# Two orders around the split of an input tile: the first three output tiles behind a norm, and the residual add of the norm behind a product

## The reference, cut to what matters

```python
h = rms_norm(x, mix_norm);  z = h @ w_in                      # product "z"
x = x + concat(o_gla, o_swa) @ w_out
h2 = rms_norm(x, ffn_norm); u = causal_dwconv(h2 @ w_up)      # product "upA"
...
u = rms_norm_2(h, mix_pre_g) @ w_pw1 + b_pw1                  # "pw1"
u = silu(layer_norm(conv(u))) @ w_pw2 + b_pw2                 # "pw2"
h = h + rms_norm_2(m, mix_post_g[layer])                      # post_norm
f = square(relu(rms_norm_2(h, ffn_pre_g[layer]) @ w_ff1)) @ w_ff2   # "ff1a0", "ff1a1"
h = h + rms_norm_2(f, ffn_post_g[layer])                      # post_norm
c_kv = rms_norm_2(rms_norm_2(h, kv_in_g) @ w_dkv, kv_norm_g)  # "dkv"
m = attention(...) @ w_o                                      # "wo"
```

## Time and profile before

| what | value |
|---|---|
| median of 3 runs | 1921.63 us (1921.1 to 1922.07) |
| span of the profiled execution | 1917.8 us |
| PE busy | 1813.4 us, 95% |
| PEld busy | 1462.6 us, 76% |
| DVE busy | 992.4 us, 52% |
| ACT busy | 628.4 us, 33% |
| POOL busy | 257.3 us, 13% |
| mean granted TensorE clock | 0.961 |

### The profile page before, as it was taken

One profiled execution on the slowest core, in us unless ns is written; L12 is line 12 of the kernel. 1 busy time (PEld: TensorE's weight loads), 2 busy tenths in 40 slices (PEclk: granted clock), 3 DMA queues, 4 the chain that ended last, 5 costly groups with the idle time before them and its releaser, 6 DMA issues.

```text
span 1917.8 us, 21982 instructions
## 1 busy us (share of the span) xinstructions
PE 1813.4 (95%) x8052; PEld 1462.6 (76%) x8052; DVE 992.4 (52%) x1290; ACT 628.4 (33%) x923; POOL 257.3 (13%) x216
## 2 busy tenths in 40 slices
PE   6999999999999999978999999988998999999996
PEld 5777978878888787857888788867666878878885
DVE  4575246663664399946542343365644374324433
ACT  4334134432343333434321222243323243112220
POOL 2100011110111122313210011120000131001111
PEclk9998799999999999968999999999889999999998
DMA  4212023332232222302332222312200213222221
GB/s 176 78 55 67 1 88 107 98 120 89 87 98 94 72 92 84 110 22 78 99 99 92 94 89 97 99 44 88 88 0 1 77 57 108 99 90 96 92 84 44
DMA packets 43841, 156.01 MB, mean 81 GB/s; under 512 B 4864, under 2 KB 4992, under 8 KB 43776
## 3 DMA queue, kind: packets, MB, share of 16 engines
q1 hardware_dynamic: 43632, 154.19, 24.5%
q10 hardware_dynamic: 144, 0.92, 0.1%
HBM read 153.00 MB, written 2.10 MB: 81 GB/s over the span
## 4 chain that ended last, share of the span: by engine, by line
PE 74%; DVE 16%; ACT 5%; issue 4%; POOL 0%; ACTq 0%; DVEq 0%; DMA 0%; POOLq 0%; SPq 0%
PE bank L991 22%; PE bank L992 21%; PE bank L993 21%; DVE cv L1832 4%; DVE w_lo L1527 3%; DVE a_lo L1545 1%; PE bank L1475 1%; ACT w_hi L600 1%; ACT w_hi L590 1%; DVE h L1901 1%; DVE m L1894 1%; DVE tmp L1758 1%; PE bank L1059 1%; PE bank L1143 1%; PE bank L1478 1%
## 5 line engine op out<-in xcount | busy, mean ns | idle before, releaser
L991 PE MATMUL bank<-a_hi,w_hi 128*128 128x512 f32 x1252 | 503.3, 402 | 49.9 <-DVE w_lo L1527 19.7
L1527 DVE TENSOR_TENSOR w_lo<-w_raw,w_hi 128x1024 fp32r<-128x1024 f32 x283 | 367.6, 1300 | 317.8 <-ACT w_hi L590 192.7
L992 PE MATMUL bank<-a_lo,w_hi 128*128 128x512 f32 x1252 | 498.7, 398 | 0.0
L993 PE MATMUL bank<-a_hi,w_lo 128*128 128x512 f32 x1252 | 496.5, 397 | 0.0
L991 PEld LDWEIGHTS bank<-a_hi,w_hi 128*128 128x128 f32 x1252 | 239.5, 191 | 116.6 <-issue 20.4
L993 PEld LDWEIGHTS bank<-a_hi,w_lo 128*128 128x128 f32 x1252 | 239.7, 191 | 52.7
L992 PEld LDWEIGHTS bank<-a_lo,w_hi 128*128 128x128 f32 x1252 | 240.0, 192 | 50.9 <-issue 0.5
L991 PE MATMUL bank<-g_hi,w_hi 128*128 128x512 f32 x688 | 269.6, 392 | 4.7 <-DVE tmp L1924 3.3
L993 PE MATMUL bank<-g_hi,w_lo 128*128 128x512 f32 x688 | 269.9, 392 | 0.0
L992 PE MATMUL bank<-g_lo,w_hi 128*128 128x512 f32 x688 | 269.1, 391 | 0.0
L590 ACT ACTIVATE w_hi<-w_raw 128x1024 fp32r<-128x1024 f32 x167 | 173.7, 1049 | 161.4 <-PE bank L993 161.3
(11 more groups left out here) (272 smaller groups left out, 1900.8 us busy)
## 6 DMA issues: line engine op xcount, KB each, us to landing
w_raw<-in_stream SPq DMA_DIRECT2D x283, 512.0 KB, 3.4
h<-in_xT SPq DMA_DIRECT2D x8, 256.0 KB, 7.0
out<-h SPq DMA_DIRECT2D x8, 256.0 KB, 2.0
cst_b<-in_consts SPq DMA_DIRECT2D x1, 896.0 KB, 9.5
cst_b<-in_consts ACTq DMA_DIRECT2D x1, 896.0 KB, 4.5
cols<-in_vectors SPq DMA_DIRECT2D x1, 289.0 KB, 2.8
cst<-in_consts SPq DMA_DIRECT2D x1, 257.0 KB, 8.4
w_al<-in_w_alpha SPq DMA_DIRECT2D x1, 128.0 KB, 10.0
```

Source lines behind the costliest of these rows:

```text
L991: pe.matmul(out, w0, x0, start=start, stop=False, skip_group_check=loose)
L992: pe.matmul(out, w0, x1, start=False, stop=False, skip_group_check=loose)
L993: return pe.matmul(out, w1, x0, start=False, stop=stop, skip_group_check=loose)
L1527: dve.tensor_tensor(w_lo[slot][:, :], w_raw[slot][:, :], f(w_hi[slot][:, :]), ALU.subtract)\
```

## The change

Two orders are changed, no arithmetic instruction is added or removed.

In `three_tiles` PE waits for the high part of tile k, issues the two products with it (w_hi x x_hi, w_lo x x_hi) for all three output tiles, then waits for the low part, and issues the three products with it (w_hi x x_lo). The last matmul of each output tile is now one of these three, and `stat` comes behind the first of them.

In `post_norm`, at the places that feed an operand, the low part of tile k - 1 is made between the scaling of tile k and the residual add of tile k. The add still waits for the scaling.

```diff
                 for k in range(8):
-                    k_ready(split, k)
+                    pe.wait_ge(xhi_ready, SPLIT0[split] + k + 1)
+                    x0, x1 = x_tile(hi, lo, k)
                     for j in range(3):
                         if k == 0:
                             unit_ready(n0 + j)
                             bank_free(name, j)
                         slot = (n0 + j) % RING
-                        last = three(bank[j][:, :], T(w_hi[slot], k, P), T(w_lo[slot], k, P), *x_tile(hi, lo, k),
-                                     k == 0, k == 7)
+                        pe.matmul(bank[j][:, :], T(w_hi[slot], k, P), x0, start=(k == 0), stop=False)
+                        pe.matmul(bank[j][:, :], T(w_lo[slot], k, P), x0, start=False, stop=False)
+                    k_ready(split, k)
+                    for j in range(3):
+                        slot = (n0 + j) % RING
+                        last = pe.matmul(bank[j][:, :], T(w_hi[slot], k, P), x1, start=False, stop=(k == 7))
                         if k == 7:
                             last.then_inc(unit_used, 1)
...
-                    link(scale)
+                    if split and k:
+                        scale.then_inc(v_chain, 1)
+                        links[0] += 1
+                        x_lo(SPLIT0[split] + k - 1, a_lo, a_hi, k - 1, T(h, k - 1), col(next_gain, ng0 + k - 1))
+                        dve.wait_ge(v_chain, links[0])
+                    else:
+                        link(scale)
                     dve.tensor_tensor(T(h, k), T(h, k), T(m, k), ALU.add)\
                         .then_inc(h_ready if split else out_ready, 1)
-                    if split and k:
-                        x_lo(SPLIT0[split] + k - 1, a_lo, a_hi, k - 1, T(h, k - 1), col(next_gain, ng0 + k - 1))
```

## The result

| | before | after |
|---|---|---|
| median of 21 runs each | 1921.33 us (1912.55 to 1928.84) | 1930.81 us (1922.58 to 1939.09) |
| ratio | | 1.0061, 95% interval 1.0044 to 1.0077 |
| span of the first profile | 1917.8 us | 1921.1 us |
| spans of two further profiles (e7, e16; e8, e15) | 1919.7, 1922.6 us | 1928.2, 1924.0 us |

The change makes the kernel slower. By the ratio it is 0.61%, that is 11.7 us (8.5 to 14.8); the two medians lie 9.5 us apart, the two means 9.9. The forecast was 5.8 us: the sign is right, the size is some half of what came, and 1930.81 lies 0.8 us outside the range. The first profile shows only 3.3 us of it; with a mean clock (the granted TensorE clock as a share of full speed, over the span) of 0.964 it was one of the quickest executions of the new kernel.

A forecast was written before the change was run, and what follows sets the result against it. PE's queue and its standstills bound the kernel; +0.72 us at PE's places and +5.03 at the three norms made +5.8, so 1921.6 us became 1927.4. The range for 8 in 10 was 1918.5 to 1930 us.

The forecast's parts named there:

- who gets the port: At the three norms, POOL's sum asks 0.11 us before the residual add and goes first; the add waits 1.04 us.
- somewhat after its shown start: POOL's request for the port may come later than shown; if by over 0.11 us, the add wins.
- the first rival: At the norms the add gets the port first, tiles in pairs of 5.51 us: 1919.5 us in all; chance 0.28.
- z: Product "z": spread 0.91 us later, two matmuls left in k = 0 for 0.46 us: +1.37 us.
- pw2: Product "pw2": six matmuls run in PE's gap before the low part of tile 0: -1.37 us.
- pw1: Product "pw1": two matmuls left over after the third bank, plus the bare spread: +0.59 us.
- the change at PE, place by place: Prices three_tiles' new order at eight calls, without the norms' DVE chain: +0.72 us with the bare spread at "upA".
- upA: Product "upA": 0.13 us behind the stat is bare; the operand order does nothing else there.
- the three norms: "ff1a0" and "ff1a1" +1.72 us each, "dkv" +1.59, from tiles every 3.19 us and bare spreads: +5.03 us.
- what a sum of POOL costs an add: At the norms, a POOL sum falling wholly before a two-input DVE operation costs DVE 1.04 us.
- a rival of 0.07: The clock falls in the norms' new gaps, 2 to 4 us more each, near 1935 us; chance 0.07.

The follow-up runs named there:

- e7: The kernel before, unchanged, run once more for a second profile: 1921.50 us.
- e16: The kernel before, unchanged, run once more for a further profile: 1924.36 us.
- e8: The changed kernel, unaltered, run once more for a second profile: 1929.99 us.
- e15: The changed kernel, unaltered, run once more for a further profile: 1925.85 us.
- e3: Changed kernel with POOL's sums at the three norms cut to 8 of 512 columns: 1920.48 us, ratio 1.0014.
- e4: Kernel before with POOL's sums at the three norms cut to 8 of 512 columns: 1917.19 us, ratio 0.9992.
- e5: Changed kernel with a one-column memset ahead of each POOL sum at the three norms: 1935.94 us, ratio 1.0078.
- e14: Changed kernel with four one-column memsets ahead of each POOL sum at the norms, 128 columns allotted for them: 1921.46 us, ratio 1.0012.
- e1: Kernel before with the new order in three_tiles alone, post_norm as before: 1922.10 us, ratio 1.0020.
- e6: Kernel before with three_tiles' new order, except k = 0 of "z" and "pw1" and k = 7 before a stat: 1919.30 us, ratio 0.9998.
- e2: Kernel before with the new order in post_norm alone, three_tiles as before: 1931.34 us, ratio 1.0081.
- e13: Changed kernel with 72 unused SBUF columns (288 bytes a partition) allotted, no instruction added: 1954.71 us, ratio 1.0181.
- e12: Changed kernel with four one-column memsets ahead of each POOL sum at the norms, 72 columns allotted for them: 1945.08 us, ratio 1.0124.

## Why the prediction was right in sign and half in size

**Right: who gets the port.** The forecast rested on POOL's sum being shown 0.11 us ahead of the add. It is 0.10 to 0.11, the sum goes first in every tile, adds are 3.25 us apart (3.19 forecast) and PE waits for the high part from the fifth tile on (third or fourth forecast). Counted from the first add of the norm, PE's first matmul comes 1.3 us earlier (1.3 forecast) and the stat 2.8 us later (2.5). e3 against e4 gives the port 7.5 of the 9.2 us. That POOL asks "somewhat after its shown start", which made the rival 0.28, is bounded by e5 and e14: it wins at 0.06 us ahead and loses at 0.00 and at 0.03 behind. So the choice between the forecast and the first rival hung on 0.05 to 0.1 us. The Trainium skill, "SBUF — State Buffer", section "SBUF: two separate sides", has the first starter hold the shared port pair for the whole instruction; these runs agree, with 1.10 us added to an add of 0.69.

**Right: "z" and "pw2".** The spread of "z" waits 1.33 us for the reciprocal (0.40 before; 1.5 forecast). PE's timeline of the changed kernel:

```profile
40.06 1.16 PE L1059 MATMUL bank<-cst,r_tok 128*128 128x128 f32 x8 [1.33 <-DVE r_tok L1557]
```

At "pw2" six matmuls at half clock stand before a gap of 1.53 us in place of the 6.05; the stage is 2.98 us shorter, 1.5 without the change in half-clock time, 1.37 forecast. Of "pw1" (0.59 forecast, 1.31 measured) nothing can be said: 1.71 of it is the column of the half-clock time.

```profile
836.17 0.79 PE L1074 MATMUL bank<-a_hi,w_hi 128*128 128x512 f32 x1 [1.59 <-ACT a_hi L866]
...
840.63 1.65 PE L1079 MATMUL bank<-a_lo,w_hi 128*128 128x512 f32 x3 [1.53 <-DVE a_lo L1548]
```

**Failed: the list of places.** The step "*the change at PE, place by place*" took eight calls, and said of "upA" that 0.13 us is bare and "the operand order does nothing else". The ninth call, "wout", isn't behind a norm and has no stat, but its output feeds a chain of DVE's that is the bound up to "upA": four matmuls later for its first tile are 0.92 us more of waiting for PE, and the stage is 2.6 us longer with the half clock that followed (0.13 forecast). This is the one place that was left out altogether.

**Too small: the three norms.** 5.03 us were forecast, 6.54 stand in the three stages. The term that fell short is what a sum of POOL costs an add: 1.04 us in the forecast, from a low part of the old order, 1.10 measured. 0.06 us too little for each of six tiles (3.25, not 3.19) makes 0.36 a norm, 1.1 of the 1.5 in all. Behind "dkv" stand 1.05 more, as the next product starts with 3.41 us at half clock in all three profiles of the changed kernel and in one of before. It does so in e1 and e6 too and not in e2, so it isn't `post_norm`'s.

**Failed: the clock and the matmuls' distance were taken as fixed.** The prediction carried the clock as a rival of 0.07 at the norms and nowhere else. Both are part of the result: 0.7 to 2 us through the mean clock, and on average of the three profiles 0.9 us through matmuls at 233.3 ns. Together: at equal clock 5.8 forecast, + 1.5 at the norms, + 0.9 at "wout", + 0.9 of distance = 9.1, of 9.2 measured; with the clock's share 10 to 11, between the 9.5 us of the medians and the 11.7 of the ratio. That 9.1 comes so near is in part luck: the last two terms are estimates from few profiles, the pairs of runs give "wout" -0.7 to +1.0 at equal clock, and the 1.5 is a difference of stages with their half-clock time in it. Shown are the port's 7.5, the 3.25 us of the loop and the 0.92 us of PE's wait.

**The range** was too narrow above for the same reason: its 1930 held only the forecast's own terms. Single runs scatter by 8 us to both sides with the clock, and a shift of the mean clock by 0.001 is worth 1.7 us. That the median missed the bound by 0.8 us says little; 9.2 us at equal clock against 5.8 says that terms were missing.

## What to carry to other kernels

Before an order is changed in a helper, list its callers from the program and not from the comment of the change; ask of each what the output's last matmul releases, not only what its input waits for. Where two engines share a port, read who asks first to 0.05 us: an order that puts a two-input operation just behind the other engine's request pays the whole of it in every tile, and a delay of 0.15 us gave 9.7 us back. Compare variants at equal mean granted clock when a few us matter, and give a test variant's scratch columns a size that doesn't move the operands' places.

## What the runs showed that wasn't expected

- The place of buffers in SBUF is worth 1.1% here (21.7 us at equal clock, e13 against the changed kernel): 288 bytes a partition more ahead of the input tiles and the large region put the matmuls at 233.3 ns instead of 228.9 nearly everywhere (e13, e12), 512 bytes do not (e14). The ring of weights didn't move. Which of the buffers that moved it is, and the rule for the offset, weren't tried.
- One kernel at one place in SBUF can have both distances: 168 us of the slower one in one of three profiles of the changed kernel.
- The scatter of one kernel's runs, some 16 us of 1920, goes nearly all with the share of time at half clock: -1.7 us per 0.001 of mean clock, in both kernels; around that line single runs scatter by 1.3 us before and 1.9 after.
